# A two-layer decoder trunk: fp32 gather straight from x, router logits with tokens in rows, and nine weight slots instead of six

## What is computed

```python
def moe_ffn(x, router_w, router_bias, w1, w3, w2):
    scores = jax.nn.sigmoid(xf @ router_w)                    # 256 x 32
    sel = (scores + router_bias).reshape(n_tok, 4, 8)
    grp = argmax(sum of the two best of each group)           # one group per token
    local = the two best experts inside grp
    gate = scores[expert] / gate.sum(-1)
    ...
    hb = jax.nn.silu(xb @ w1[e]) * (xb @ w3[e])               # for each of 32 experts
    return hb @ w2[e]                                         # added to the token, times gate
...
for layer in range(2):
    mix = attention_mixer(...) if layer == 0 else gdn_mixer(...)
    x = layer_norm(ALPHA * x + mix)
    x = layer_norm(ALPHA * x + moe_ffn(x))
```

## Time and profile before

| | us |
|---|---|
| median of 3 runs (lowest, highest) | 1583.29 (1582.74, 1584.98) |
| the profiled execution, its own time | 1582.79 |
| its span from first to last instruction | 1581.0 |

### The profile page before, as it was taken

The page is one execution under the profiler, slowest core; times in us unless marked ns, Lnnn a source line. Parts: engine busy times, 40 slices in busy tenths (PEclk is TensorE's granted clock), DMA queues, the critical chain, the costliest instruction groups (busy, mean ns, idle before and its releaser), DMA issues. The chain is left out here.

```text
span 1581.0 us, 40565 instructions
## 1 busy us (share of the span) xinstructions
PE 1202.8 (76%) x17935; PEld 891.0 (56%) x17935; DVE 457.4 (29%) x1369; ACT 274.8 (17%) x676; POOL 34.8 (2%) x42
## 2 busy tenths in 40 slices
PE   8999676666666666799989899997866666666664
PEld 4444464554554554588888887543655555455553
DVE  1344511111111111465656544313211111111113
ACT  1232200000000000235244346202000000000000
POOL 0000300000000000000000000002000000000000
PEclk9999799999999999899999999998899999999998
DMA  9620599999999999943300001405799999999995
GB/s 362 243 107 16 196 425 426 427 425 426 429 425 426 428 426 423 355 160 107 129 32 1 1 28 55 157 4 236 313 427 426 425 427 427 426 425 428 425 427 234
DMA packets 63246, 461.77 MB, mean 292 GB/s; under 512 B 3872, under 2 KB 4016, under 8 KB 30416
## 3 DMA queue, kind: packets, MB, share of 16 engines
q1 hardware_dynamic: 61680, 455.90, 70.2%
q0 software_dynamic: 1504, 5.00, 0.9%
HBM read 459.83 MB, written 1.05 MB: 292 GB/s over the span
## 5 line engine op out<-in xcount | busy, mean ns | idle before, releaser
L711 PE MATMUL bank<-ring,arena 128*32 128x128 f32 x8192 | 311.0, 311 | 282.8 <-DMA ring<-in_moe_w 280.1
L711 PEld LDWEIGHTS bank<-ring,arena 128*32 128x32 f32 x8192 | 268.9, 123 | 332.9 <-DMA ring<-in_moe_w 241.3
L1009 ACT ACTIVATE arena<-bank 128x512 f32<-128x512 f32 (+3 forms) x294 | 128.9, 456 | 342.0 <-PE bank L680 97.9
L1485 DVE SCALAR_TENSOR_TENSOR arena<-arena,bank 128x128 f32<-128x128 f32 x64 | 18.4, 288 | 503.8 <-ACT arena L1085 503.8
L1085 ACT ACTIVATE arena<-bank 128x128 f32<-128x128 f32 x64 | 17.8, 278 | 691.9 <-PE bank L711 691.9
L725 PE MATMUL bank<-ring,arena 128*32 128x256 f32 x2048 | 124.4, 382 | 5.2 <-DMA ring<-in_moe_w 3.5
L765 PE MATMUL bank<-xT,ring 128*128 128x256 f32 x512 | 115.6, 385 | 0.0
L765 PEld LDWEIGHTS bank<-xT,ring 128*128 128x128 f32 x512 | 98.5, 194 | 16.5 <-issue 3.3
L677 PEld LDWEIGHTS bank<-arena 128*128 128x128 bf16 x3072 | 89.8, 97 | 11.1 <-issue 10.3
L677 PE MATMUL bank<-arena 128*128 128x32 bf16 x3072 | 87.0, 177 | 10.1 <-DVEq L1459 8.3
L725 PEld LDWEIGHTS bank<-ring,arena 128*32 128x32 f32 x2048 | 63.8, 109 | 47.6 <-issue 14.4
(11 more groups left out here) (218 smaller groups left out, 1122.0 us busy)
## 6 DMA issues: line engine op xcount, KB each, us to landing
ring<-in_moe_w SPq DMA_DIRECT2D x192, 2048.0 KB, 26.5
ring<-in_gdn_w_in SPq DMA_DIRECT2D x12, 2048.0 KB, 14.9
ring<-in_ab_w_in SPq DMA_DIRECT2D x5, 2048.0 KB, 24.0
ring<-in_gdn_w_out SPq DMA_DIRECT2D x4, 2048.0 KB, 8.0
ring<-in_ab_w_out SPq DMA_DIRECT2D x2, 2048.0 KB, 19.9
ring<-in_ab_w_in SPq DMA_DIRECT2D x2, 1024.0 KB, 8.6
x<-in_x SPq DMA_DIRECT2D x2, 512.0 KB, 4.9
arena<-in_mix_ln_g POOLq DMA_DIRECT2D x2, 512.0 KB, 5.4
```

What stands on the lines that cost most here:

```text
L711: last = mm(psum[5][h * CAP:(h + 1) * CAP, m * FH:(m + 1) * FH], xeT[:, j], ring[:, slots[m], j, h // 2 * SEQ + h % 2:(h // 2 + 1) * SEQ:2 ...
L1009: return do(o, i, ACT.Copy, **kw)
```

## The change

- **Slots.** `SLOTS = 9`: the ring's six, and three more of 16 KB per partition in `arena` at 24, 40 and 56 KB (`spare`). `slot_att`, `slot_gdn` and `slot_moe` say where a unit goes; GDN and attention still use the ring alone. An expert's units now wait for the expert three places earlier (`freed`). In MoE 0 four units wait for projections as before and five for `mix_ps` at 4; in MoE 1 two wait for z projections, five for `mix_ps` at 12, two for `x_ready` at 6 (the norm behind GDN).
- **Loops.** The pattern of nine slots and two buffers repeats after six experts: PE's and SP's loops get `GROUP = 6` experts per pass (5 passes, then two experts written out).
- **Gather.** `xs`, `res` and the work on ACT and POOL for them are gone; the gather takes fp32 `x` as the stationary operand, with `pick` in fp32: 8 x 2 = 16 products per expert instead of 48.
- **Logits.** Tokens in rows: `xT` is the stationary operand and `rw` streams, 2 x 8 products; the copy to `lgT` and the transposes back are gone. Token tile 0 is transposed, copied and multiplied before token tile 1 (its transposes no longer wait for `mix_ps`). The last of the four PSUM banks of `xT` is copied by DVE (`last_xT`) and not by ACT, also for attention and GDN. GDN's output goes to banks 4 to 7 (`GDN_OUT`), so that banks 0 to 3 are free.
- **Tables.** Only the first copy of `pos` and `gate` is made in `route`; the other seven are made if the second pass runs. The memsets of `y_e` and `gpT` are put ahead of the wait for the logits. The flag is made behind the first picks, and PE and ACT wait for it behind the experts.
- The tiles of the MoE move to the first 14 KB of `arena`, the layer norms' tables to 16 KB (GDN's stay at 48), `wba` and `ab` get memory of their own.

```diff
@@ load_experts (SP) @@
+                def freed(n):
+                    def wait(m):
+                        sp.wait_ge((s.w1_used, s.h_ps, s.y_ps)[m], n + (s.e + 1 - DEPTH))
+                    return wait
+
+                for n in range(DEPTH):
+                    load_expert(n, n, lambda m: first_free(3 * n + m))
+                for n in range(DEPTH, GROUP):
+                    load_expert(n, n, freed(n))
+                with sp.Fori(1, NE // GROUP) as i:
+                    for c in range(GROUP):
+                        load_expert(i * GROUP + c, c, freed(i * GROUP + c))
+                for n in range(NE // GROUP * GROUP, NE):
+                    load_expert(n, n % GROUP, freed(n))
...
+            def free_for_moe0(u):
+                if u < 4:
+                    sp.wait_ge(proj_ps, 2 * (u + 2) + 2)
+                else:
+                    sp.wait_ge(mix_ps, 4)
...
+            def free_for_moe1(u):
+                if u < 2:
+                    sp.wait_ge(z_ps, 2 * u + 6)
+                elif u < 7:
+                    sp.wait_ge(mix_ps, 12)
+                else:
+                    sp.wait_ge(x_ready, 6)
@@ router (PE) @@
-                transpose_x(1 + 2 * layer)
-                for j in range(DJ):
-                    pe.wait_ge(xT_sb, 4 * (1 + 2 * layer) + j // 2 + 1)
-                    last = mm(psum[4][0:NE, 0:SEQ], rw[:, j], xT[:, j], start=(j == 0), stop=(j == DJ - 1))
-                last.then_inc(lgT_ps, 1)
-                pe.wait_ge(lgT_sb, layer + 1)
+                n = 1 + 2 * layer
                 for t in range(NT):
-                    last = transpose(psum[5][:, t * NE:(t + 1) * NE], lgT[0:NE, t * P:(t + 1) * P], ident[0:NE, 0:NE])
+                    transpose_x(n, t)
+                    if t == 0:
+                        pe.wait_ge(xT_sb, 3 * n + 2)
+                        pe.wait_ge(y_sb, 2 * n)
+                    for j in range(DJ):
+                        if t:
+                            xT_ready(n, j)
+                        last = mm(psum[5][:, t * NE:(t + 1) * NE], xT[:, j, t * P:(t + 1) * P], rw[:, j],
+                                  start=(j == 0), stop=(j == DJ - 1))
@@ gather, experts (PE) @@
-                        for part in range(3):
-                            mm(psum[4][:, j * CAP:(j + 1) * CAP], xs[:, t, part, j], pick[:, b, t],
-                               start=(t == 0 and part == 0), stop=(t == NT - 1 and part == 2))
+                        mm(psum[4][:, j * CAP:(j + 1) * CAP], x[:, t, j::DJ], pick[:, b, t],
+                           start=(t == 0), stop=(t == NT - 1))
...
-                with pe.Fori(0, steps // 2 - 1) as i:
-                    turn(i, False)
-                turn(steps // 2 - 1, True)
+                whole = (steps - 1) // group
+                with pe.Fori(0, whole) as i:
+                    turn(i, range(group), False)
+                turn(whole, range(steps - whole * group), True)
...
-                pe.wait_ge(xs_sb, 2 * (layer + 1))
-                pe.wait_ge(flag_sb, layer + 1)
-                experts(fast[layer], slot_full, NE, u0)
+                experts(fast[layer], slot_full, NE, lambda u: slot_moe(layer, u), MOE_BASE[layer], SLOTS)
+                pe.wait_ge(flag_sb, layer + 1)
@@ moe (ACT) @@
-                for t in range(NT):
-                    act.wait_ge(x_ready, 4 * layer + 1 + t)
-                    copy(xs[:, t, 0], x[:, t].rearrange("p (q j) -> p j q", j=DJ)).then_inc(part_act, 1)
-                act.wait_ge(lgT_ps, layer + 1)
-                copy(lgT[0:NE], psum[4][0:NE, 0:SEQ]).then_inc(lgT_sb, 1)
@@ last_xT, route (DVE) @@
+            def last_xT(n):
+                dve.wait_ge(xT_ps, 4 * n + 4)
+                v.tensor_copy(xT[:, 4:8, P:SEQ], psum[3][:].rearrange("p (j t) -> p j t", j=4)).then_inc(xT_last, 1)
```

More of the change, by code:

```diff
@@ L78, with slot_att, slot_gdn, slot_moe @@
 RING = 6
-UNIT_ATT = 0
-UNIT_MOE0 = UNIT_ATT + 8
-UNIT_GDN = UNIT_MOE0 + 3 * NE
-UNIT_MOE1 = UNIT_GDN + 16
+SLOTS = 9
+DEPTH = SLOTS // 3
+GROUP = 6
+GDN_OUT = 4
+def slot_att(u):
+    return (u + 4) % RING
+def slot_gdn(u):
+    return u % RING
+MOE_SLOTS = ((0, 1, 2, 3, 4, 5, 6, 7, 8), (4, 5, 0, 1, 2, 3, 6, 7, 8))
+def slot_moe(layer, u):
+    return MOE_SLOTS[layer][u % SLOTS]
+def fill_counts():
+    n = [0] * SLOTS
+    att, gdn, moe = [], [], []
+    def fill(slot):
+        n[slot] += 1
+        return n[slot]
+    for u in range(8):
+        att.append(fill(slot_att(u)) if u else 0)
+    for layer in range(2):
+        moe.append(list(n))
+        for u in range(3 * NE):
+            fill(slot_moe(layer, u))
+        if layer == 0:
+            for u in range(16):
+                gdn.append(fill(slot_gdn(u)))
+    return att, gdn, moe
+ATT_FILL, GDN_FILL, MOE_BASE = fill_counts()
 COLS = {}
@@ L693, in scatter, with experts, turn @@
                 return last
-            def experts(s, fulls, steps, first):
-                def turn(i, ends):
-                    for b in range(2):
-                        n = i * 2 + b
-                        slots = [(first + 3 * b + m) % RING for m in range(3)]
-                        filled = [i * 16 + 16 * ((first + 3 * b + m) // RING + (1 if slots[m] or fulls is not slot_full else 0))
+            def experts(s, fulls, steps, slot_of, base, size):
+                group = 2 if size == RING else GROUP
+                def turn(i, cs, ends):
+                    for c in cs:
+                        n, b = i * group + c, c % 2
+                        ends_here = ends and c == cs[-1]
+                        slots = [slot_of(3 * c + m) for m in range(3)]
+                        filled = [i * (16 * 3 * group // size) + 16 * (base[slots[m]] + (3 * c + m) // size + 1)
                                   for m in range(3)]
@@ L751, in gdn @@
             def gdn():
-                transpose_x(2)
+                for t in range(NT):
+                    transpose_x(2, t)
                 def project(n):
@@ L1385, in route @@
                 own(v.memset(gsum, NEG))
+                own(v.memset(y_e, 0.0))
+                own(v.memset(gpT[:, 1], 0.0))
+                last_xT(1 + 2 * layer)
                 dve.wait_ge(sc_sb, layer + 1)
@@ L1433, in route, with experts @@
                 dve.wait_ge(rank_ps, layer + 1)
-                own(v.tensor_reduce(out=cnt, in_=psum[6][:, 2 * NE:3 * NE], axis=AX, op=ALU.max))
                 own.link(v.scalar_tensor_tensor(out=t32, in0=psum[6][:, 0:2 * NE].rearrange("p (t e) -> p t e", t=NT),
                                                 scalar=1.0, in1=both, op0=ALU.add, op1=ALU.mult))
-                for q in range(PASSES):
-                    own(v.tensor_scalar(out=pos[:, :, q * NE:(q + 1) * NE], in0=t32, scalar1=-1.0 - q * CAP,
-                                        scalar2=None, op0=ALU.add))
-                dve.wait_ge(init, 1)
-                v.tensor_copy(flag[:, layer, 0:1], cnt).then_inc(flag_sb, 1)
-                own.wait()
-            def experts(s, steps, base):
+                own.link(v.tensor_scalar(out=pos[:, :, 0:NE], in0=t32, scalar1=-1.0, scalar2=None, op0=ALU.add))
+            def experts(layer, s, steps, base):
                 o2 = Own(dve, s.own)
@@ L1470, in experts @@
                 picks(0, 0)
+                if not base:
+                    o2.link(v.tensor_reduce(out=cnt, in_=psum[6][:, 2 * NE:3 * NE], axis=AX, op=ALU.max))
+                    dve.wait_ge(init, 1)
+                    o2(v.tensor_copy(flag[:, layer, 0:1], cnt))
+                    o2.wait()
+                    dve.sem_inc(flag_sb, 1)
                 dve.wait_ge(s.gathered, 1 + s.e)
@@ L1503, in moe @@
                 route(layer)
-                experts(fast[layer], NE, 0)
+                experts(layer, fast[layer], NE, 0)
                 dve.wait_ge(flag_sb, layer + 1)
@@ L1508, in moe @@
                     dve.wait_ge(fast[layer].scattered, 1 + fast[layer].runs)
-                    experts(more[layer], NIT - NE, NE)
+                    experts(layer, more[layer], NIT - NE, NE)
                     dve.wait_ge(more[layer].scattered, 1)
```

259 lines of the change are left out of this document (123 added, 136 removed).

## The result

The changed kernel takes 1790.99 us (median of 4 runs, 1787.9 to 1791.71) beside 1584.13 us for the kernel before on the same chip (4 runs, 1582.74 to 1586.35): 1.130 times the time, 95% interval 1.128 to 1.132, or 206.9 us more. The forecast was 1562.4 us, range 1553.5 to 1571.0. It was wrong, and in sign too.

The account below looks back on a forecast made before the run. The experts' weight stream (DMA) was taken to bound the kernel: 1582.79 less 28.1 us of idle gaps plus 7.2 us for code fetches is 1561.9, with 0.5 for the median 1562.4 us; range 1553.5 to 1571.0.

Parts of the forecast that it names:

- Gather in fp32: PE's gather per expert: 0.96 to 3.74 us for 32 fp32 records, 2.6 taken, +1.2 us, off the path.
- another one, on bf16 and fp32: Trainium skill's rule weighed for the gather: fast weight load is for 128 columns of types other than fp32; no size given.
- By either end the sum is unchanged.: In the expert blocks, a gather of 0.96 or 3.74 us alike leaves the forecast time unchanged.
- The fetches: PE's loop of six experts fetches its code every pass: 51 more pieces a layer, 1.1 us each, 7.2 us altogether.
- Are they spread?: Whether code pieces fall on all 16 DMA engines: yes, 3.6 us a layer; on one engine, 57 us.
- The rival in which the pieces fall on half of the engines: Code fetches in the expert loops cost twice as much: +7.2 us, 1569.6; chance 0.15, shared with a half-open layer-0 gap.
- PE's waits for code: In the expert loops, waits of a few tenths to two us a piece fall into PE's 5 us slack per expert.
- The slower rival: PE becomes the bound by its code in the expert loops: at 4 us a piece, 1700 us; chance 0.08.
- Slots: Between mixers and experts, three more units loaded early fill the stream's idle time: 14.8 us layer 0, 9.7 us layer 1.
- Router: Before layer 0's experts, routing about 7 us earlier, 4.7 us of it from three steps without POOL's split of x.
- the release: Layer 0's first w1 is used up at 184 us, not 190.6, before the stream's work ends at about 187.
- Sum of the right terms: Whole kernel with idle gaps closed (28.1 us), gather hidden, no added code fetches: 1555.2 us; as a rival, chance 0.20.

Follow-up runs that it names:

- experiment 12: Changed kernel with three experts per pass and the gather reading a copy of x with weights 16 bytes apart: 1751.85 us.
- experiment 5: Changed kernel with the gather reading an unstrided fp32 copy of x, and passes of three experts instead of six (third buffers): 1557.62 us.
- experiment 6: Changed kernel, strided fp32 gather kept, with passes of three experts instead of six: 1751.09 us.
- 10: Changed kernel with a 48-product bf16 gather on unstrided data (lower parts of x left out) and passes of three experts: 1555.08 us.
- experiment 3: Kernel before with only PE's loop lengthened, six experts per pass instead of two: 1605.13 us.
- 7: Kernel before with only PE's loop lengthened, four experts per pass instead of two: 1606.17 us.
- 1: Changed kernel with only the gather altered, reading an unstrided fp32 copy of x made by ScalarE: 1578.86 us.
- experiment 4: Changed kernel with a 48-product bf16 gather on unstrided data (lower parts of x left out), passes of six kept: 1576.49 us.
- experiment 9: Changed kernel with unstrided fp32 gather and passes of three experts, its nine slots filled only six units ahead: 1578.14 us.
- experiment 8: Changed kernel with unstrided fp32 gather and passes of three experts, plus GpSimd's four old subtractions beside the router, result unused: 1573.84 us.

## Why the prediction was wrong, point by point

- **The step that failed: "Gather in fp32", its upper end.** I bounded the record by line 866 (3.74 us for 32) and took 2.6. The row has the type and the size of the load, but its weights lie side by side; those of line 729 lie 32 bytes apart. Measured 7.70 us. Unstrided it is 3.66, so the row was right for what it showed, and its form missed the one thing that decided. The rule was there to be read (experiment 12), and the prediction weighed another one, on bf16 and fp32, in its place.
- **"By either end the sum is unchanged."** True of the two ends that I had, but the term lay outside them. With 7.70 us it isn't: 8.4 + 7.7 - 1.44 = 14.7 us, level with the stream's 14.75. What tips it is a term I didn't have: PE's clock. While it ran the slow gather, the granted clock fell from 1.00 to 0.50, and w2 behind it took 3.64 instead of 1.93 us, line 732 0.67 instead of 0.42: 16.6 us, against the 16.72 read. Eight us of work came into 6.4 us of slack (14.75 less 8.4). With the unstrided gather w2 also takes 3.64 us in some experts (experiment 5 has both values), but there the slack holds it. No run has the slow gather at full clock throughout, so the clock's share is read from the rows and has no experiment of its own. I should have asked what the clock does when PE has more to do. Experiments 6 and 10 differ by the gather (and ScalarE's copies for it beside the router) and by 196.0 us.
- **The fetches.** The count held (150 pieces, 145 forecast; 45 and 2 x 51 are 147). The price of one was right in time on an engine (0.9% for 39 pieces in 300 us is 1.1 us each), and "Are they spread?" was wrong: four pieces of a first pass were too few to answer it. The landings of experiment 3 show eight of 16 engines falling behind. Measured 18.5 to 21.4 us (experiments 3 and 7, 1 less 5, 4 less 10) for 7.2. The rival in which the pieces fall on half of the engines had 0.15 together with others and twice the price, 14.4 us. It is what the landings look like, at 2.6 to 3 times my price; with the 1.5 us a piece of experiment 3 (an estimate, its cause open) instead of 1.1 the rival's sum is 19.6 us. With the gather unstrided the sum would have given 1562.4 and been wrong by 14 to 16 us for this reason alone, just out of my range.
- **PE's waits for code** "fall into its 5 us of slack": true where there is slack (experiments 1 and 4), worth 40 us where there is none (experiment 6). The slower rival had PE as the bound by its code, at over 2.8 us a piece; PE did become the bound, but by the gather, and code added 0.6 us an expert.
- **Slots.** I gave 14.8 us in layer 0 and 9.7 in layer 1, 24.5 in all (18.4 less 14.8 leaves 3.6 us to the router there, not the 3.4 that I wrote). Measured 20.5 (experiment 9): layer 1 gave less, since with the faster router w1 comes back 28.7 us after SP's issues there (1083.85 to 1112.50), and in the kernel before after 33.0.
- **Router.** The 4.7 us put down to GpSimd's work were its doing (0.2 us steps after; experiment 8), and the release would have come at 184: it did in experiment 4 (184.51). In the kernel after, the first gather of 7.82 us ate all of it.
- **Sum of the right terms.** 1555.2 forecast without fetches and with a hidden gather, 1555.1 measured. That they meet to 0.1 us is luck: the five runs lie between 1550.14 and 1563.16, and the kernel before took 1586.10 beside them, so 31.0 us were gained where 28.1 were forecast; where the other 3 us come from is open. From there to the change as made it is 196.0 us for the strided gather and 39.9 for the fetches at the seams; these are differences of the same runs, so that they lead to 1791.0 is no proof of its own.

## What to carry to other kernels

Before bounding an operand's cost by a row, compare its access pattern too, not only type and shape: here fp32 weights 16 or 32 bytes apart took twice as long to go through a gather as those 4 or 8 bytes apart. An engine's slack must hold the added work and what the lower clock then does to the rest. And the length of a loop's body has a price of its own on a kernel bound by DMA: choose buffer counts so that the period stays short, here three of each instead of the common multiple of two and three.

## What was not expected of the hardware

- A 128x128 fp32 load with weights 16 or 32 bytes apart goes at 0.24 us a record at full and at half clock; with 4 or 8 bytes it takes 0.11 to 0.12 us at full clock.
- Loops that fetch their code split the 16 DMA engines' parts of a transfer into eight early and eight late: with 52 pieces of 16 KB between 215 and 600 us they drift from 2 to over 11 us apart, and the stream lost 2.4% where the pieces' own time was 0.9%. That the pieces fall on the late eight is inferred.
- A loop of 1266 matmul and load records stays on the core (one piece in 300 us), one of 1816 doesn't (34).
- Beside GpSimd's subtractions, DVE's two-input steps took 7 to 13 times as long, its reductions and maxima as long as ever.
